# Reordering the ends of the expert and second output products, and constant TensorE products ahead of the norms, in a two-block transformer kernel

## The reference

```python
# first block, layer l
h = rms_norm(x, norm_mix[l]) * (1 + sc_a) + sh_a          # sc, sh, g: rows of silu(c) @ w_mod[l] + b_mod[l]
x = x + g_a * (concat(moba_attention, diff_attention)(h @ w_in[l]) @ w_out[l])
h = rms_norm(x, norm_ffn[l]) * (1 + sc_f) + sh_f
x = x + g_f * ((silu(h @ w_gate[l]) * (h @ w_up[l])) @ w_down[l])
# second block, layer l
x = x + head_group_mixer(rmsnorm(x, mix_norm[l]), ...)    # stick-breaking heads, retention heads with a group norm
x = x + memory_cross_attn(rmsnorm(x, xa_norm[l]), rmsnorm(mem, mem_norm[l]), ...)
x = x + peer_ffn(rmsnorm(x, peer_norm[l]), ...)
```

## Time and profile before

| | us |
|---|---|
| median of 3 runs | 2905.5 (2903.01 to 2906.28) |
| the profiled execution | 2902.05 |
| its span in the profile | 2900.3 |
| TensorE busy | 2791.4 |
| VectorE busy | 2090.9 |
| ScalarE busy | 1408.0 |
| mean granted clock of TensorE | 0.98 |

### The profile page before, as it was taken

How to read it: one execution, slowest core, us unless ns; L and a number is a source line. 1 busy time by engine, 2 the same in 40 slices (tenths; PEclk the granted TensorE clock), 3 DMA queues, 4 the chain that set the end, 5 groups by cost and what they waited for, 6 DMA issues and landing times. The chain is left out here.

```text
span 2900.3 us, 40006 instructions
## 1 busy us (share of the span) xinstructions
PE 2791.4 (96%) x16468; PEld 2382.6 (82%) x16468; DVE 2090.9 (72%) x3086; ACT 1408.0 (49%) x1620; POOL 192.0 (7%) x168
## 2 busy tenths in 40 slices
PE   6989999999999999999999999998999999999998
PEld 6768888788888788888878888887888888888887
DVE  6777866665543669989879955435599989699755
ACT  4554445554456445554444444484445544444443
POOL 0200001000003001110000000030011200000000
PEclk9989999999999999999999999999999999999999
DMA  8747854545543355554445555533445544455554
GB/s 320 288 174 272 311 206 168 202 167 192 192 180 131 117 174 175 189 174 162 173 160 189 175 189 195 217 126 121 157 163 189 189 160 163 158 192 174 186 193 148
DMA packets 75637, 537.41 MB, mean 185 GB/s; under 512 B 8512, under 2 KB 8896, under 8 KB 12096
## 3 DMA queue, kind: packets, MB, share of 16 engines
q1 hardware_dynamic: 75456, 534.86, 52.7%
HBM read 527.48 MB, written 7.34 MB: 184 GB/s over the span
## 5 line engine op out<-in xcount | busy, mean ns | idle before, releaser
L946 ACT ACTIVATE whi<-raw 128x2048 fp32r<-128x2048 f32 x438 | 838.6, 1915 | 985.9 <-issue 827.6
L1396 DVE TENSOR_TENSOR wlo<-raw,whi 128x2048 fp32r<-128x2048 f32 x438 | 1006.3, 2298 | 331.0 <-ACT whi L946 330.3
L428 PE MATMUL banks<-ht,whi 128*128 128x512 f32 x3136 | 771.5, 395 | 7.4 <-DVE big L1470 5.4
L428 PEld LDWEIGHTS banks<-ht,whi 128*128 128x128 f32 x3136 | 576.5, 189 | 123.3 <-issue 6.9
L503 PE MATMUL banks<-whi,ht 128*128 128x512 f32 x1152 | 459.6, 399 | 18.2 <-DVE ht L1460 10.0
L505 PE MATMUL banks<-whi,ht 128*128 128x512 f32 x1152 | 452.7, 393 | 0.0
L436 PEld LDWEIGHTS banks<-ht,wlo 128*128 128x128 f32 x3136 | 401.9, 191 | 15.8
L436 PE MATMUL banks<-ht,wlo 128*128 128x256 f32 x3136 | 406.6, 283 | 0.0
L513 PE MATMUL banks<-wlo,ht 128*128 128x512 f32 x1152 | 287.4, 389 | 0.0
L503 PEld LDWEIGHTS banks<-whi,ht 128*128 128x128 f32 x1152 | 218.6, 190 | 65.3 <-issue 19.3
L505 PEld LDWEIGHTS banks<-whi,ht 128*128 128x128 f32 x1152 | 218.7, 190 | 44.3
(11 more groups left out here) (259 smaller groups left out, 3263.6 us busy)
## 6 DMA issues: line engine op xcount, KB each, us to landing
raw<-in_pu SPq DMA_DIRECT2D x128, 1024.0 KB, 4.9
raw<-in_pv SPq DMA_DIRECT2D x128, 1024.0 KB, 4.9
raw<-in_win SPq DMA_DIRECT2D x52, 1024.0 KB, 4.9
big<-in_wmod SPq DMA_DIRECT2D x24, 1024.0 KB, 6.4
raw<-in_wmod SPq DMA_DIRECT2D x24, 1024.0 KB, 4.9
raw<-in_wgate SPq DMA_DIRECT2D x22, 1024.0 KB, 4.9
raw<-in_wup SPq DMA_DIRECT2D x22, 1024.0 KB, 4.9
raw<-in_wdown SPq DMA_DIRECT2D x22, 1024.0 KB, 4.9
```

Of the source, the lines that this page charges most:

```text
L428: m = e.matmul(bank[b + n], h[:, q, c[n]], M.both[:, q * 512:(q + 1) * 512], start=q == 0, stop=False, skip_group_check=True)
L946: e.activation(whi(j), slot[u][0], ACT.Copy).then_inc(*hi.mark(j))
L1396: e.tensor_tensor(wlo(j), slot[u][0], whi(j).bitcast(F32), ALU.subtract).then_inc(*lo.mark(j))
```

## The change

1. `warm` (new) issues n products of the constant identity with the constant 128 x 256 block (identity and counting numbers) into bank 7, which nobody reads, ahead of `turn_all` in the first mixer of layer 0 (7), the second mixer (9, in layer 1 six), cross attention (6) and peer (6).
2. `gate_row`'s two products move from behind `turn_all` into `modulation`, after 5 and 11 of its 16 products, in the first mixer of layer 1 and in both feed forwards.
3. Unit `a` 0 moves between query unit 7 and the eighth head's scores, on all engines.
4. The slot transposes take banks 0 and 1 instead of two of the rotating banks; the gates begin at unit 33 instead of 32, and `pace` gives two at units 33, 37, ... instead of 32, 36, ...
5. Between the two expert products, ScalarE and VectorE split the gated values 0 before they move out unit 63, and ScalarE splits 1 before the last activation.
6. In the second mixer VectorE takes the mean of the retention output from PSUM, ahead of its rest for the first pair, and subtracts it on the way out of PSUM; ScalarE's two copies are gone, and VectorE's next remainder comes behind the subtraction instead of before the mean.

```diff
     def pace(u):
-        return 2 if u % 4 == 0 else 1
+        return 2 if u % 4 == 1 else 1
...
+        def warm(name, n, b=7):
+            clear(("warm", *name), b)
+            on.wait_ge(*d_const.at(0))
+            for _ in range(n):
+                e.matmul(bank[b][:, 0:256], IDN, SM[:, 0:256], start=True, stop=True)
...
             for q in range(16):
+                if between is not None and q in (5, 11):
+                    between(q // 11)
                 m = e.matmul(bank[b][:, q:q + 1], sums[q], ONES[:, 0:1], start=True, stop=True)
...
             name = ("ffn", l)
-            modulation(l, 1)
+            modulation(l, 1, None, lambda q: gate_row(l, 1, (0, 1), (q,)))
             turn_all(name, XA, DG[0])
-            gate_row(l, 1, (0, 1))
...
             name = ("mix2", l)
+            warm(name, 6 if l else 9)
             turn_all(name, XA, DG[0])
...
             for i in range(9):
-                if i < 8:
-                    wide_unit(("pq", l, i), HT, ready)
+                wide_unit(("pq", l, i) if i < 8 else ("a", l, 0), HT, ready)
...
-                        b = clear(("top", l, t))
+                        b = clear(("top", l, t), t)
...
-                due = plan.step(pace(u))[0] if GATES <= u < 58 else []
+                due = plan.step(pace(u))[0] if GATES < u < 58 else []
...
+            for u in range(1, 64):
+                if u == GATES - 1:
+                    exponent()
+                k = take()
+                upto(k + 2)
+                gelu(u - 1)
+                if u == 63:
+                    mm1 = k
+                    split_weights(0)
+                region(on, l, u)
+                apart(ag(u * 512, 512), ("a", l, u), k)
+            split_weights(1)
+            gelu(63)
...
+            raw = [psum(("ov", l, 2 + t))[:, :].rearrange("p (n d) -> p n d", n=4) for t in range(2)]
+            on.wait_ge(*valued.at(("ret", l, 3)))
             for t in range(2):
-                on.wait_ge(*took_a.at(("ov", l, 2 + t)))
-                e.tensor_reduce(mu[:, t * 4:t * 4 + 4], ov[t], X, ALU.add).then_inc(*normal.mark(("o2", l, "sum")))
+                e.tensor_reduce(mu[:, t * 4:t * 4 + 4], raw[t], X, ALU.add).then_inc(*normal.mark(("o2", l, "sum")))
+            out_parts(("o2", l), l, (0, 1))
```

More of the change, by code:

```diff
@@ L388, in clear, with modulation @@
             return b
-        def modulation(l, part, b=None):
+        def warm(name, n, b=7):
[3 more added lines that the diff above has]
+                e.matmul(bank[b][:, 0:256], IDN, SM[:, 0:256], start=True, stop=True)
+        def modulation(l, part, b=None, between=None):
             if part == 0:
@@ L1240, in second_mixer @@
             upto(used[0] + 1)
-            for t in range(2):
-                key = ("ov", l, 2 + t)
-                on.wait_ge(*valued.at(("ret", l, 3)))
-                e.copy(os[t][:, 512:1024], psum(key)[:, :]).then_inc(*took_a.mark(key))
             head_squares(("o2", l, 1), [o[:, 512:1024] for o in os], sqs,
-                         lambda t: on.wait_ge(*normal.at(("o2", l, "mean", t))))
+                         lambda t: on.wait_ge(*took_v.at(("ov", l, 2 + t))))
             take()
@@ L1321, in peer @@
             for i in range(9):
+                k = take()
+                since()
                 if i < 8:
-                    k = take()
-                    since()
                     apart(ag(QT + i * 512, 512), ("pq", l, i), k)
+                else:
+                    region(on, l, 0)
+                    apart(ag(0, 512), ("a", l, 0), k)
                 if i:
@@ L2029, in peer @@
             for i in range(9):
-                if i < 8:
-                    take()
+                take()
                 if i:
@@ L2038, in peer @@
             plan = Gates()
-            for u in range(64):
+            for u in range(1, 64):
                 if u == 58:
@@ L2065, in peer @@
             split_weights(0)
+            activated(63)
             plan = Gates()
```

50 lines of the change are left out of this document (20 added, 30 removed).

## The result

The changed kernel takes 2865.7 us in the median of four runs (2863.95 to 2869.78), beside 2904.26 (2902.06 to 2906.28) for the kernel before, timed with it: a ratio of 0.9872 (0.9858 to 0.9885), 38.6 us less. The profiled execution took 2865.42 us, its span is 2863.7, and the mean granted clock rose from 0.980 to 0.987. The forecast was 2871 for the median and 2868 for the profiled execution.

What follows compares the result with a forecast made beforehand. TensorE was taken as the bound, with only its idle time and half-rate clock to win. The steps summed to 37.2 us, 34 after 3.2 for new falls: 2871 us median, range 2863 to 2891.

Steps and rivals of the forecast that it cites:

- new falls: Anywhere in the kernel: two new clock falls behind short waits that remain, 3.2 us held back from the gain.
- F: Gate row products inside the modulation, three stages: L541 starts 1.88 later, partly given back; net 1.5 us lost.
- C: Second expert product: splitting weights before unit 63 cuts PE's wait to 1.87 and keeps the clock up; 7.2 us gained.
- D: Second mixer's end: mean taken from PSUM, so waits shrink by 1.55 per layer and clock holds; 6.3 us gained.
- A: Expert stage: unit 0 before the eighth score hides the 2.99 us wait for VectorE's join; 7.6 us gained.
- second and third rivals: Expert units: join waits return, about 2879 (chance 0.08); or VectorE falls behind and sets the pace, 2911 or more (0.03).
- B: Slot transposes in banks 0 and 1: unit 32's 2.68 us wait and its clock cost go; 8.7 us gained.
- E: Constant products before seven norms: they hold the clock for the transposing products behind; 9.2 us gained, start's share 0.
- G: One-hot pace one unit later: PE may wait a few tenths for VectorE before unit 58; 0.3 us lost.
- The first rival: Whole kernel: the clock part is not won, only idle time less two feed forwards' loss, 14.7 us: 2891 (chance 0.17).

Runs made afterwards that it cites:

- e3: Changed kernel with the six later blocks of constant products (not the first mixer's seven) made one column wide, about twice as many products: 2876.51 us, ratio 0.9906.
- e12: Changed kernel, gate rows still inside the modulation, with the modulation's 16 products multiplying by 128 columns of ones instead of one: 2868.20 us, ratio 0.9892.
- e9: Changed kernel with gate rows back behind the turning passes and the modulation's products by 128 columns of ones instead of one: 2856.08 us, ratio 0.9841.
- e1: Changed kernel with only the gate row products put back behind the turning passes: 2858.76 us, ratio 0.9857.
- e4: Changed kernel without the block of seven constant products in the first mixer of layer 0: 2864.82 us, ratio 0.9872.
- e10: As e9, with VectorE making the diagonal matrices before it takes the modulation's sums instead of after: 2854.57 us, ratio 0.9842.

## Why the prediction was right, and where it was not

**The time** came out 5.3 us below the forecast and within its range. The six single edits undone add up to 33.0 by their medians (8.1 + 7.3 + 6.7 + 9.2 + 8.6 - 6.9) of the 38.6. By the ratios, each to the kernel before timed with it, they are 9.6, 7.0, 7.0, 9.6, 8.4 and -4.4, together 37. Each of the six is uncertain by about 5, so what is left over says nothing.

By stretches, of the profiled executions: the rest was forecast at 34.0 (idle time 18.2, clock 20.6 less 1.6 for the start in the middle and 3.2 for the new falls) and gave 34.5, 16.7 of it idle time and 17.7 clock. The middle was forecast at +0.1 and gave -0.6. The start, forecast at 0, gave 2.7, which lies within its spread. The mechanism, idle time and clock in about equal parts, is borne out. That the sum is so near is in part luck: F and C's clock were put too high, and against them D was put too low and the 3.2 held back for new falls were not needed.

**A, C: right.** 8.1 and 6.7 by the medians, forecast 7.6 and 7.2. VectorE kept up: PE waits for no join in the expert units, so the second and third rivals did not occur. C's wait is 2.00 for a forecast of 1.87. The forecast that the clock stays up behind it held in layer 1 and not in layer 0, so 1.6 of its 7.2 did not come in this trace; in eight others, with the same wait in layer 0, it did. With A undone the clock falls behind its wait in both layers, and not in layer 1 alone as in the kernel before.

**B: right, with the next wait mis-sized.** 7.3 for 8.7. The step said that the slot gates keep a margin of 0.1 to 0.2 us; they are 0.34 late in each layer, 0.7 us in all. The low part ahead of them took 2.86 beside GpSimd's products, which A had put one unit later; with A undone the margin holds.

**D: mechanism right, too small.** 9.2 for 6.3. The idle time came as forecast: 3.05 (1.06 + 1.99) became 1.50 (1.55). The mis-sized term is the clock, forecast at 1.6 a layer. From the retention scores to cross attention's L549 the version with D undone takes 4.7 us longer in layer 0 and 3.6 in layer 1; less 1.5 of idle time that leaves 3.2, where half rate lasted 6.8 us, and 2.0, where it lasted 3.4.

**E: right in size and in cause.** 8.6 for 9.2. The 6.68 and the four stretches of 5.22 to 5.47 are now 3.84, and e3 shows that it is the wide products and not any work in the wait that do it. The start's share was forecast as 0 and is 0.

**F: the step that failed.** Forecast 1.5 lost, measured 5.1 in the middle of one pair of traces (4.4 against the mean of the six). The prediction had the order of things (the columns wait for the last sum, L541 0.87 behind it), and then said "if the clock stays up, the first quarter of L541 gives back (6.75 - 3.84)/4 = 0.7". The clock did not stay up in any of the three places: L549 takes 6.57, 6.77 and 6.79 (L541 took 6.75, 5.73 and 6.37 there before), and in feed forward 0 it starts 3.45 us later behind the start (18.91 for 15.46), where 1.88 was forecast. The gate rows are 512 columns wide, but the one-column products around them are not. The clock is not the whole of it, though. With the clock up (e12 beside e9) the order still costs 4.5: 1.7 in each feed forward where 1.2 was forecast, so nothing is given back, and 1.1 in the mixer of layer 1, where a gain of about 1 was forecast. Its unit does give back 0.5, but not the 1.7 by which it starts later. How much of the measured 5.1 is clock cannot be told, since half rate and waiting for the pieces hide each other there.

**G** showed no wait. **The two new falls** (3.2) did not come: in the rest the only fall is the one behind C's wait in layer 0, where the kernel before had one too.

**The first rival and the page's rule.** The first rival did not occur: the clock gave 17.7 us in the rest, and the constants alone, which save no other time, are worth 8.6. In the kernel before, PE is busy for 100.5 us at half rate; half of that, an estimated 50 us, is what it cost, 1.7% of the span. The Trainium skill (TensorE: Matmul & The Clock Gate, Part 1) has the ramp below 1% of a typical span; this kernel, whose clock falls in 23 places, lies above it. Its other half, that the number of slow products varies from run to run, the traces bear out: the fall in the second product of layer 0 comes in some traces and not in others, with the same wait of 2.00 ahead of it.

## What to carry to other kernels

A wait of TensorE has two prices, the idle time and the clock behind it; read both from the timeline, and price a filler by the clock alone. Fill with wide products or make the work that stands there wide: 16 sums of one column or of 128 took 3.63 and 3.73 us here, and only the second kept the clock. A clock that stays up is worth time only where PE is what the stage waits for: in the feed forwards part of it turned into a longer wait. Before work is moved into a wait, ask what its neighbours wait for: the modulation looked like filler for the norm, but VectorE's queue tied the diagonal to its end, so what was put into it came out at the end.

## What the runs showed that was not expected

- Products of one column, for which PE is busy 2.60 of 2.60 us, let the clock fall to half rate behind them as an empty wait does; 256 columns in the same wait keep it at 1.00.
- 16 sums by 128 columns take 3.73 us, by one column 3.63 at full clock: the width was nearly free.
- The same code before 220 us ended from 218.10 (A undone) to 224.01 (B undone) in eight traces. The stretch from the retention scores of layer 0 to the start of its expert stage is 166.71 to 166.77 in nine (the changed kernel, A, B and C undone, e1, e4, e10 to e12). So the times spread by the first 220 us and by single falls.
- A VectorE low part took 2.86 instead of its mean of 2.30 while GpSimd worked on 128x256 products, and 2.29 with A undone, where GpSimd was done by then. Moving a unit for TensorE had brought the two together.
